# A block of transformer layers in split fp32: one order of the tokens for all projections in place of two

## The reference

```
h = rmsnorm(x, norm_mix_g)
z = h @ w_in                       # 1024 -> 5888 columns
qa, ka, va, qb, kb, vb, ga, gb = split(z)
y_a = mixer_a(qa, ka, va) @ w_out_a
y_b = mixer_b(qb, kb, vb, rel_bias) @ w_out_b
x = x + (sigmoid(ga + b) * y_a + sigmoid(gb + b) * y_b) @ w_out
```

## Time and profile before

| | |
|---|---|
| time, median of 3 runs | 2131.89 us (2131.61 to 2133.17) |
| profiled execution: its own time, its span | 2131.61 us, 2129.8 us |
| mean granted TensorE clock | 0.993 |
| PE busy | 2081.2 us (98%) |
| PEld, weight loads | 1749.8 us (82%) |
| DVE busy | 1170.8 us (55%) |
| ACT busy | 865.9 us (41%) |
| POOL busy | 328.2 us (15%) |
| DMA | 198.62 MB, mean 93 GB/s |

### The profile page before, as it was taken

How to read it: one execution, slowest core, us unless ns; L and a number is a source line. 1 busy time by engine, 2 the same in 40 slices (tenths; PEclk the granted TensorE clock), 3 DMA queues, 4 the chain that set the end, 5 groups by cost and what they waited for, 6 DMA issues and landing times.

```text
span 2129.8 us, 26955 instructions
## 1 busy us (share of the span) xinstructions
PE 2081.2 (98%) x10562; PEld 1749.8 (82%) x10562; DVE 1170.8 (55%) x2216; ACT 865.9 (41%) x1644; POOL 328.2 (15%) x526
## 2 busy tenths in 40 slices
PE   8999999999999999999999999999989999999998
PEld 7777888888888888878888889878878888888887
DVE  6676546575444344674543445666755665444445
ACT  6556344354423233543322324544444443332324
POOL 2311000021000001221110113312532011110101
PEclk9999999999999999999999999999999999999999
DMA  5141432123323333223333322212242123332223
GB/s 173 53 131 60 117 84 82 60 69 99 107 93 98 99 99 99 80 84 96 98 99 99 99 87 97 70 65 90 92 137 80 60 80 99 99 99 91 94 83 129
DMA packets 197879, 198.62 MB, mean 93 GB/s; under 512 B 3820, under 2 KB 193068, under 8 KB 197676
## 3 DMA queue, kind: packets, MB, share of 16 engines
q1 hardware_dynamic: 197752, 196.89, 29.3%
HBM read 194.66 MB, written 6.93 MB: 95 GB/s over the span
## 4 chain that ended last, share of the span: by engine, by line
PE 88%; DVE 3%; POOL 3%; issue 3%; ACT 2%; DMA 0%; SPq 0%; DVEq 0%; POOLq 0%; ACTq 0%
PE ps L601 24%; PE ps L607 24%; PE ps L604 24%; PE ps L610 2%; PE ps L613 2%; PE ps L616 2%; POOL m L693 1%; PE ps L1102 1%; PE ps L1391 1%; DVE m L641 0%; ACT m L632 0%; PE ps L1859 0%; PE ps L1382 0%; POOL m L1679 0%; POOL m L819 0%
## 5 line engine op out<-in xcount | busy, mean ns | idle before, releaser
L601 PE MATMUL ps<-m,m 128*128 128x512 f32 (+1 forms) x2432 | 951.0, 391 | 2.0 <-ACT m L890 2.0
L607 PE MATMUL ps<-m,m 128*128 128x512 f32 (+1 forms) x2432 | 939.5, 386 | 0.0
L604 PE MATMUL ps<-m,m 128*128 128x512 f32 (+1 forms) x2432 | 938.9, 386 | 0.5 <-DVE m L641 0.5
L632 ACT ACTIVATE m<-m 128x512 fp32r<-128x512 f32 x688 | 400.0, 621 | 579.3 <-PE ps L607 545.8
L641 DVE TENSOR_TENSOR m<-m,m 128x512 fp32r<-128x512 f32 x688 | 512.4, 762 | 64.3 <-ACT m L632 60.7
L601 PEld LDWEIGHTS ps<-m,m 128*128 128x128 f32 x2432 | 458.1, 188 | 94.4 <-issue 5.4
L607 PEld LDWEIGHTS ps<-m,m 128*128 128x128 f32 x2432 | 457.7, 188 | 94.0 <-DVE m L912 1.2
L604 PEld LDWEIGHTS ps<-m,m 128*128 128x128 f32 x2432 | 458.3, 188 | 87.1 <-DVE m L641 0.7
L1596 POOL TENSOR_TENSOR m<-m,m 128x512 f32<-128x512 f32 x44 | 76.2, 1732 | 492.7 <-DVE m L1573 492.7
L610 PE MATMUL ps<-m,m 128*128 128x256 f32 x512 | 151.7, 296 | 0.3 <-ACT m L2194 0.3
L613 PE MATMUL ps<-m,m 128*128 128x256 f32 x512 | 146.7, 287 | 1.5 <-DVE m L641 1.4
(11 more groups left out here) (333 smaller groups left out, 1966.2 us busy)
## 6 DMA issues: line engine op xcount, KB each, us to landing
m<-ffn_w SPq DMA_DIRECT2D x60, 1024.0 KB, 5.3
m<-w_ff SPq DMA_DIRECT2D x32, 1024.0 KB, 5.4
m<-w_in SPq DMA_DIRECT2D x28, 1024.0 KB, 5.2
m<-ffn_w SPq DMA_DIRECT2D x12, 768.0 KB, 4.5
m<-w_in SPq DMA_DIRECT2D x17, 512.0 KB, 5.1
m<-w_out SPq DMA_DIRECT2D x8, 1024.0 KB, 5.2
m<-mem_w_kv SPq DMA_DIRECT2D x8, 1024.0 KB, 5.5
m<-w_out_a SPq DMA_DIRECT2D x4, 1024.0 KB, 5.1
```

The lines of the kernel that those rows point to most:

```text
L601: pe.matmul(o, lh, xh, start=k == 0, stop=False)
L604: pe.matmul(o, ll, xh, start=False, stop=False)
L607: done = pe.matmul(o, lh, xl, start=False, stop=k == nk - 1)
L632: act.activation(self.WH[b % 2][:, at], self.RAW[b % 2][:, at], ACT.Copy).then_inc(*self.up("w_hi", b, c))
```

## The change

The "class" version of x is no longer made. `act_remake`, `dve_remake` and their places go, and all jobs from `qkb0` to `gb` use the "mix" version, which lies in token order. Where the class order is needed, it is made elsewhere:

- q/k jobs come out in token order. `dve_classed` reads bank and RB contiguously and writes `tmp` through `by_class`: the element of token 4l + r goes to place 128r + l, so consecutive elements lie 512 bytes apart, four at a time.
- the value jobs get `permuted=True`: their stationary operand is class i of x, picked by `class_of` from the tokens in order, 128 floats with a step of 16 bytes.
- the gates of `gb` are in token order throughout and use the operation of the `ga` gates, L1208.

```diff
-def classes(ap):
-def classed(ap):
+def by_class(ap):
-    return ap.rearrange("p (r l) -> p r l", r=4)
+    return ap.rearrange("p (r l) -> p l r", r=4)
...
-                                 [Job(("qkb", pair, g), xc, 0, P, j_b), Job(("qkb", pair, 3 + g), xc, P, P, j_b)]))
+                                 [Job(("qkb", pair, g), xg, 0, P, j_b), Job(("qkb", pair, 3 + g), xg, P, P, j_b)]))
...
-                         [Job(("vb", pair, r), xc, 0, 256, j_b, tiles=(r, r + 1)) for r in (0, 2)])]
+                         [Job(("vb", pair, r), xg, 0, 256, j_b, tiles=(r, r + 1), permuted=True) for r in (0, 2)])]
...
-                                 [Job(("vb3", r), xc, 0, 256, j_b, tiles=(r, r + 1)) for r in (0, 2)]))
+                                 [Job(("vb3", r), xg, 0, 256, j_b, tiles=(r, r + 1), permuted=True) for r in (0, 2)]))
...
-        self.stage("gb", [feat(w, GB + P * j, "gb", xc, j_b, (j, j + 1)) for j in range(0, 8, 2)])
+        self.stage("gb", [feat(w, GB + P * j, "gb", xg, j_b, (j, j + 1)) for j in range(0, 8, 2)])
...
-                    o, xh, xl = out[:, n * job.width:(n + 1) * job.width], x.hi[k][:, i * P:(i + 1) * P], x.lo[k][:, i * P:(i + 1) * P]
+                    pick = (lambda ap: class_of(ap, i)) if job.permuted else (lambda ap: ap[:, i * P:(i + 1) * P])
+                    o, xh, xl = out[:, n * job.width:(n + 1) * job.width], pick(x.hi[k]), pick(x.lo[k])
...
-            dve.tensor_tensor(classes(dst[:, j, :]), classed(self.bank((name, j))), classes(self.RB[:, :]), ALU.mult).then_inc(
-                *self.drained((name, j)))
+        dve.tensor_tensor(dst[:, j, :], self.bank((name, j)), self.RB[:, :], ALU.mult).then_inc(*self.drained((name, j)))
...
-    def act_remake(self, act, new):
-    def dve_remake(self, dve, new):
...
-            dve.scalar_tensor_tensor(out=classed(slot), in0=classed(self.bank(name)), scalar=0.125, in1=classes(self.RB[:, :]), op0=ALU.mult,
+            dve.scalar_tensor_tensor(out=by_class(slot), in0=self.bank(name), scalar=0.125, in1=self.RB[:, :], op0=ALU.mult,
                                      op1=ALU.mult).then_inc(*self.drained(name))
         else:
-            dve.tensor_tensor(classed(slot), classed(self.bank(name)), classes(self.RB[:, :]), ALU.mult).then_inc(*self.drained(name))
+            dve.tensor_tensor(by_class(slot), self.bank(name), self.RB[:, :], ALU.mult).then_inc(*self.drained(name))
```

More of the change, by code:

```diff
@@ L188, with __init__ @@
 class Job:
-    def __init__(self, name, operand, col, width, banks, tiles=None, ks=None, half=None, block=None, begun=None):
+    def __init__(self, name, operand, col, width, banks, tiles=None, permuted=False, ks=None, half=None, block=None, begun=None):
         self.name, self.operand, self.col, self.width, self.banks = name, operand, col, width, banks
-        self.tiles, self.ks, self.block, self.begun = tiles, ks, block, begun
+        self.tiles, self.permuted, self.ks, self.block, self.begun = tiles, permuted, ks, block, begun
         self.tokens = slice(0, S) if half is None else slice(256 * half, 256 * half + 256)
@@ L222, in class_of @@
     return ap.rearrange("p (l r) -> p r l", r=4)[:, r]
-def classes(ap):
-    return ap.rearrange("p (l r) -> p r l", r=4)
-def classed(ap):
-    return ap.rearrange("p (r l) -> p r l", r=4)
+def by_class(ap):
+    return ap.rearrange("p (r l) -> p l r", r=4)
 def by_token(x):
@@ L341, in memory @@
         made = lambda v: ((lambda k: self.at("xg_hi", v, k)), (lambda k: self.at("xg_lo", v, k)))
-        self.xg = {v: Operand(*xg, *made(v)) for v in ("mix", "class", "mlp", "both", "mx2", "mq", "f2")}
+        self.xg = {v: Operand(*xg, *made(v)) for v in ("mix", "mlp", "both", "mx2", "mq", "f2")}
         self.TG = pa(0, [P, 8, S])
@@ L459, in plan_first @@
     def plan_first(self):
-        w, xg, xc, cycle = self.io["w_in"], self.xg["mix"], self.xg["class"], self.cycle
+        w, xg, cycle = self.io["w_in"], self.xg["mix"], self.cycle
         feat = self.feature_block
@@ L1206, in dve_gates @@
             dve.wait_ge(*w)
-        if name == "ga":
-            dve.tensor_tensor(dst[:, j, :], self.bank((name, j)), self.RB[:, :], ALU.mult).then_inc(*self.drained((name, j)))
-        else:
-            dve.tensor_tensor(classes(dst[:, j, :]), classed(self.bank((name, j))), classes(self.RB[:, :]), ALU.mult).then_inc(
-                *self.drained((name, j)))
+        dve.tensor_tensor(dst[:, j, :], self.bank((name, j)), self.RB[:, :], ALU.mult).then_inc(*self.drained((name, j)))
     def act_sigmoids(self, act, new, name, dst, bias, places):
@@ L1257, in act_constants @@
         act.activation(self.lam_e, self.dots, ACT.Exp).then_inc(*self.up("lam_e"))
-    def remake_place(self, t):
-        return self.start["oa"] + 0.1 + 0.42 * t
-    def act_remake(self, act, new):
[L1265 to L1270, removed]
-    def dve_remake(self, dve, new):
[L1273 to L1280, removed]
     def qkb_block(self, pair, n):
@@ L2652, in scalar @@
         s += [self.act_sigmoids(act, new, "ga", self.TG, G_BG, [b["oa"] - 0.3 + (0.055 if j < 7 else 0.1) * j for j in range(8)])]
-        s += [self.act_remake(act, new)] + [self.act_classed(act, new, pair, n) for pair in range(2) for n in range(6)]
+        s += [self.act_classed(act, new, pair, n) for pair in range(2) for n in range(6)]
         s += [self.act_values(act, new, ("vb", pair, r), mix, made, [self.filled(("oa", 7)) if pair == 0 else self.filled(("pv_b", 0, 7))],
@@ L2699, in vector @@
         s += [self.dve_gated_a(dve, new, j, b["oa"] + 0.5 * j + 0.55) for j in range(8)]
-        s += [self.dve_remake(dve, new)] + [self.dve_classed(dve, new, pair, n) for pair in range(2) for n in range(6)]
+        s += [self.dve_classed(dve, new, pair, n) for pair in range(2) for n in range(6)]
         s += [self.dve_values(dve, new, ("vb", pair, r), mix, b["vb0"] + 0.25 * r + 0.62 if pair == 0 else b["vb1"] + 0.89 + 0.13 * r, self.vb_parts(pair, r))
```

## The result

The changed kernel takes 2164.06 us (median of 4, 2162.9 to 2165.72) against 2131.97 us of the kernel before, a ratio of 1.015 with a 95% interval of 1.0135 to 1.0167: 32.1 us slower. The profiled execution took 2165.28 us with a span of 2163.5.

A forecast was written before the change was run, and what follows sets the result against it. PE was taken as the bound, busy without waits from 209.3 to 460 us. Profiled 2131.6 + 32.8 (strided loads) + 0 + 0 = 2164.4, about 2164.7 beside the median; range 2152 to 2174.

The forecast's parts named there:

- No slack in the stage: From 209.3 to 460 us PE is always busy and waits for nobody; whatever lengthens its stream goes straight to the end.
- The price of a load: Value jobs, 288 strided weight loads: 0.234 us each in place of 0.120, 32.8 us in all; bounds 0 and 41.5.
- The rival by which the loss is a number of PE's cycles: Same 288 loads: 280 cycles in place of 256, 0.122 us each, 0.6 us in all, 2132.2; chance 0.14.
- The pace is that of the slower of load and matmul: Value jobs: the 256-column matmul, 0.107 us, runs beside the next load, so the loads set the pace.
- Zero for the removed remake: Between 212 and 247 us: 9.6 us off ACT and 9.1 off DVE are worth 0 us, since PE has no wait.
- zero for the cheaper gates: Eight `gb` gates on DVE go from 1090 to 682 ns, 3.3 us off DVE, hidden behind PE.
- `dve_classed` unchanged and hidden: Its twelve DVE operations stay at 1.07 us, hidden by 4.4 us of slack before their bank is wanted again.
- The clock: PE's granted clock was expected not to fall to 0.5 between 287 and 400 us, because PE is never idle here.
- 1 us hidden by the attention's longer matmuls: A dozen value loads beside interleaved attention matmuls hide up to 0.1 us each, giving back 1 us, left to the range.
- The rival of the falling clock: During load-bound stages the clock falls; strided loads stay 0.234 us, interleaved attention and q/k jobs pay: up to 2222; chance 0.03.

The follow-up runs named there:

- the wide matmuls: Changed kernel with each strided load followed by a 512-column matmul in place of 256, half of the slices left out: 2134.29 us, ratio 1.0009 against the kernel before.

## Why the prediction was right

- **No slack in the stage.** PE busy for the whole of the windows, before and after, and no wait: every microsecond of loads reached the end. The kernel with the strided loads alone shows it by 32 us, in a place more than 1700 us from the end.
- **The price of a load.** Taken as 0.234 us from L710's loads at 1.2 GHz, measured 0.233 at 2.4 GHz; 288 x 0.113 = 32.5 us against the forecast sum of 32.8 and 32.1 in the medians. The rival by which the loss is a number of PE's cycles asked for 0.12 us at 2.4 GHz and falls. The value has the same nanoseconds at both clocks, and the steps of 8, 12, 16 and 32 bytes show what sets it: about 1.8 ns for each 16-byte line. The prediction had one piece for each element, which at 16 bytes is the same number, 128. It had also placed the limit in the memory; the runs show a limit in time that counts lines, not where it lies. The Trainium skill names such lines in "Advanced Engine Details and Errata" (SBUF Cachelines), and these runs agree with it. The rule of the Trainium skill's "TensorE: Matmul & The Clock Gate" (LDWEIGHTS) that a load's time depends on its columns alone is borne out here for steps up to 8 bytes (0.112 and at most 0.120 us); at 16 bytes it gives 107 ns where 0.233 us were measured.
- **What was luck in it.** The price came from one place, six loads at 1.2 GHz, where the limit was just above the 0.213 us of contiguous loads; had it lain below, that row would have shown nothing. That it is a limit in time was argued from DVE and ACT, and weakly: the pairs of rows behind their 1.94 and 2.06 ns mix operations that write with the step (L1440, L1464) with ones that read with it (L1278, L1269), and neither value is the 1.82 ns of a load. It took the runs to show it.
- **The pace is that of the slower of load and matmul.** Assumed in the sum, shown by the wide matmuls: a strided load sets 0.233 us with 256 columns and 0.235 with 512, so the 0.113 us are not added to the matmul's own time.
- **Zero for the removed remake, zero for the cheaper gates.** Right within some 2 us: the kernel without the strided loads stands at 0.9999.
- **`dve_classed` unchanged and hidden.** Forecast 1.07 us, measured 1.09 and 1.10; no wait came of it.
- **The clock.** It stayed at 2.4 GHz from 205 to 490 us, as forecast. But the reason given, that PE is never idle there, is not enough to keep it there: see the last section.
- **1 us hidden by the attention's longer matmuls.** Neither shown nor excluded; it is under what these measurements tell.

No version that beats the kernel before came out of this. What the change saves lies on engines PE doesn't wait for, and the kernel without its one cost is no faster.

## What to carry to other kernels

Before a copy that orders data is replaced by a stride in the operand, look at who reads that operand: on ACT and DVE, with time to spare, a step of 16 bytes cost the end nothing here; in the stationary operand of a stage in which loads already filled nine tenths of the pace it nearly doubled the stage, from 0.120 to 0.233 us a load. Count the 16-byte lines that a load touches, at some 1.8 ns each, and compare with the pace of the matmul that follows: with up to 8 bytes between floats the stride cost nothing here (0.120 us), and with 512 columns to a load next to nothing (0.235 us, where such matmuls have 0.227). And an operation's price at another clock can be taken from a row only once it is known whether it is limited in cycles or in time; similar nanoseconds on three engines pointed to time, and the step of 32 bytes, with 0.242 us at either clock, shows it.

## What the runs showed of the hardware that was not expected

The granted clock can fall while TensorE is busy without a gap. In the profiled execution of the kernel with a step of eight floats it did so twice. PE alone: stretch, length, busy us (instructions), clock, DMA share, GB/s.

```profile
300.00:319.40 19.40, 19.40 (x84) 1.00 0.20 54
319.70:322.80 3.10, 3.10 (x14) 0.50 0.02 5
323.20:340.00 16.80, 16.80 (x76) 1.00 0.23 62
...
405.10:408.20 3.10, 3.10 (x15) 0.50 0.03 5
```

Ahead of each fall lie runs of loads at 0.242 us, each with a matmul of 256 columns (whose pace is 0.120 us with contiguous loads). The last work before it are nine attention matmuls (their loads start from 317.50 to 318.75 us, and from 402.54 to 403.81) and three or four more strided loads. In the profiled execution of the changed kernel, with 0.233 us and the same order of work, the clock stayed up. Its other executions have mean clocks of 0.990 to 0.994, against 0.992 in the profiled one, so falls in some of them can't be excluded, and what brings one about is not shown. These loads don't notice the clock. In the low stretch:

```profile
319.71 0.34 PEld L611 LDWEIGHTS ps<-m,m 128*128 128x128 f32 x1
...
322.62 0.34 PEld L611 LDWEIGHTS ps<-m,m 128*128 128x128 f32 x1
```

Twelve loads in 2.91 us, 0.242 each, as at 2.4 GHz: within one execution, a limit in time. Both low stretches hold value loads alone, so these falls cost nothing that shows. The rival of the falling clock was right that a strided load takes as long at either clock; the argument held against it, that PE is never idle here, doesn't rule it out.
